# Expert up-projection with products of 448 columns, its halves added afterwards

## The chip, the cores and the metric

One core of one Trainium2 chip. The metric is the device time of one execution in microseconds (us); lower is better. The core's engines each work through a queue of their own: TensorE (PE, matrix products; PEld is its weight load), VectorE (DVE), ScalarE (ACT), GpSimd (POOL) and SyncE (SP, which here issues transfers). They wait for each other by semaphores.

## The reference

Two transformer blocks, one after the other, over 256 tokens of 1024 features. The change lies in the first block's expert layer (PEER). Each token gets 16 of 16384 experts from each of eight heads; an expert is a row of `peer_u` and a row of `peer_v`:

```
def expert_block(args):
    ht, it, gt = args
    ue = jnp.take(u, it, axis=0)
    act = jax.nn.gelu(jnp.einsum('tkd,td->tk', ue, ht), approximate=False)
    ve = jnp.take(v, it, axis=0)
    return jnp.einsum('tk,tkd->td', gt * act, ve)
```

## The kernel before

**Split products.** Every float32 operand a is cut into a high part a_h (rounded to the fast matmul type) and a low part a_l = a - a_h. A product a b is made as a_h b_h + a_h b_l + a_l b_h, three matrix products into one bank of PSUM; `three` issues them. The weight comes in *units* of 128 x 1024 values: SyncE loads a unit into one of four buffers `raw`, ScalarE makes its high part (`hi`, into one of three buffers `whi`, line L1234), and VectorE (`lo`, L1829) or GpSimd (L2777) makes the low part (`wlo`). Unit i's `hi` waits until TensorE has finished unit i - 3 (semaphore `w`).

**The expert layer is dense.** All 16384 experts are computed for 224 of the 256 tokens (`TD`; the first 32 tokens are done with gathered rows). The up-projection has 128 units ("u", unit 0 to 127), each 128 experts. TensorE works a unit in eight steps k (blocks of 128 features), each of them three products of 224 columns, the weight's part being loaded and the tokens' part `hT` being streamed: `whi` with the high tokens, `whi` with the low tokens, `wlo` with the high tokens. Two units share one bank, and three banks (4, 5, 6) take turns. ScalarE then applies GELU to both units of a bank at once (448 columns), into the buffer `acts` (inside `A2`, "A" in the profile). The down-projection ("v") follows, again 128 units; there `down` uses, for six of eight k, one product of 448 columns that streams both halves of the tokens' operand, and accumulates them in one place for each half; it adds the halves at the very end.

**Work beside it.** While TensorE does the up-projection, VectorE does the routing: `routing(0)` and then `routing(1)`, a generator each, cut into 30 pieces. Each engine's program steps its generators once per unit (twice in units 12, 26, 40 and 54, `U1_STEPS`), so a piece stands at a fixed place in the queue, but nothing except semaphores holds engines at the same unit. A routing is: the 16 largest of 128 for 16 rows (maxima, replacing them, maxima again, their indices; pieces 1 to 10), candidate sums (11), the 16 largest of 256 for eight rows (12 to 21), small conversions (22), the selection of indices by one-hot products and reductions (23 to 26), and normalised gates (27), for which ScalarE makes an exponential in piece 22. TensorE transposes the results after unit 27 and unit 55, and VectorE copies them (`iT`). In units 0 to 51 GpSimd makes the low parts, from then on VectorE. From unit 50 on GpSimd issues gathers for the first 32 tokens, and VectorE makes products with the gathered rows (`pick_u`; in unit 51 it also scales a row of tokens). From unit 70 on VectorE builds one-hot matrices in groups (`gates`), one group for two units, and TensorE multiplies them.

Of the kernel before, what the change touches and what calls it, by code (L numbers as in the profile page):

```python
# [7 lines left out]
ALU = mybir.AluOpType  # L8
ACT = mybir.ActivationFunctionType
# [29 lines left out]
NGRP = TD // OB  # L39
EARLY = 10  # L40
G_DENSE = 70
REP_AT = 51
DOT_AT = [55 + 3 * g // 2 for g in range(EARLY)] + [71 + 2 * (14 * g // 11) for g in range(NPK - EARLY)]
ACC_AT = [57 + 2 * g for g in range(NPK)]
# [125 lines left out]
hd_pe hd_act hd_dve hd_pool mask xv_ev cr_pe cr_act cr_dve  # L170
ff_a ff_c ff_g ff_h ff_lo
own_act own_dve own_pool zeros x_sq hi_half lo_half lo_first f_xg f_xd f_act hd_mask
pk_idx pk_rep pk_used pk_act v_tile v_b v_sum v_tr x_g
""".split()


# [37 lines left out]
def build(nc, x, mem, wdram, keep_d, con0_d, con1_d, con2_d, keys_d, w2c_d, gf_d, gf2_d,  # L214
          gffn_d, utab, out):
    ctx = ExitStack()
    with ctx:
# [25 lines left out]
        iota_b = sb("iota_b", P * 2, F16)  # L243
        zero_b = sb("zero_b", P, BF16)
        first_cut = sb("first_cut", 4 * T, F32R)

        with ExitStack() as c:
            A1 = sb("A1", 24576, c=c)
# [135 lines left out]

        def cut(part, n):
            return both_cuts(n)[:, part, :]

        v_banks = (0, 1, 2, 3, 5, 6, 4, 4)
        out_banks = ((7, 0), (1, 2))
# [77 lines left out]
        def pe_program(e):  # L467
# [136 lines left out]
            def lin_T(u0, units, src, K, first=None, after=None, steps=(1,), c0=0):  # L604
                per = KD // K
                for u in range(units):
                    i = u0 + u
                    wv = [z.rearrange("p (n k c) -> p n k c", n=per, k=K) for z in unit(i)]
                    for j in range(per):
                        n = u * per + j  # L610
                        q = pair[0]
                        bk = 4 + q % 3
                        if n % 2 == 0:
                            use(bk)
                        for k in range(K):
                            if n == 0 and first:
                                first(k)
                            ins = three(banks[bk][:, (n % 2) * 256:(n % 2 + 1) * 256 - c0], [z[:, j, k, :] for z in wv],
                                        [z[:, k, c0:T] for z in src], k == 0, k == K - 1)
                            if 2 * (j * K + k + 1) == KD:  # L620
                                mid.step()
                        if n % 2:
                            by, n_ev = PAIR_FREED[q]
                            free[bk] = (s[by], n_ev)
                            pair[0] += 1
                    ins.then_inc(s["w"], 1)
                    if after:
                        after(u)
                    side.step(steps[(i + 1) % len(steps)])

            def lin_A(u0, src, K, N, bks, ready, pair=True, split=None):
# [460 lines left out]
                    ins.then_inc(s["sc_pe"], 1)  # L1092
                    free[g] = (s["sc_act"], 4 * b + g + 1)
            side.lists[0] += [routing(0), routing(1)]
            lin_T(BASE["u"], 62, hTv, KD, steps=U1_STEPS, c0=NG)
            side.drain()
            lin_T(BASE["u"] + 62, G_DENSE - 62, hTv, KD, c0=NG)
            side.lists[0] += [gates(0), gates(1)]
            lin_T(BASE["u"] + G_DENSE, P - G_DENSE, hTv, KD, c0=NG)

            def down(n, w, k):
                bk, o = banks[v_banks[k]], v_cols(k) + NG
# [125 lines left out]
        def act_program(e):  # L1228
# [449 lines left out]
                    act(hrep[q, :], hrep[0:NG, :], ACT.Copy).then_inc(s["pk_rep"], 1)  # L1678

            side.lists[0] += [routing(0), routing(1)]  # L1680
            lin_T(BASE["u"], 62, gelu(0), rep_h, steps=U1_STEPS)
            side.drain()
            def first_cuts(u):
                if u == 64:
                    cut_acts(0)
                    cut_acts(1)

            lin_T(BASE["u"] + 62, 66, gelu(62), first_cuts)
            e.wait_ge(s["pk_used"], NPK)
            act(pk_co, pk_dot, ACT.Gelu).then_inc(s["pk_act"], 1)  # L1690
            for n in range(128):
# [123 lines left out]
        def dve_program(e):  # L1815
# [848 lines left out]
            own(e.tensor_copy(banks[7][:, 0:16], K_("iota16")))  # L2664
            own(e.tensor_copy(t3(iota_b[:, :], P), K_("iota").unsqueeze(2).to_broadcast([P, P, 2])))
            side.lists[0] += [routing(0), routing(1)]
            lin_T(BASE["u"], 62, before=pick_u, steps=U1_STEPS)
            side.drain()
            lin_T(BASE["u"] + 62, G_DENSE - 62, before=lambda u: pick_u(u + 62))
            side.lists[0] += [gates(0), gates(1)]  # L2670
            lin_T(BASE["u"] + G_DENSE, P - G_DENSE, before=lambda u: pick_u(u + G_DENSE))
            cut_acts(0)
            cut_acts(1)
            for n in range(128):
# [425 lines left out]
```

## Time and profile before

| | |
|---|---|
| median of three runs | 1383.48 us (1383.48 to 1385.43) |
| profiled execution | 1383.28 us, its span 1381.2 us |
| TensorE busy | 1357.3 us, 98% of the span |
| VectorE busy | 1037.8 us, 75% |
| ScalarE busy | 737.3 us, 53% |
| GpSimd busy | 292.4 us, 21% |

The span is the time from the first to the last instruction on the core; the execution's own time is 2.1 us longer. Busy time counts an engine's instructions once, where they overlap. A single product's length includes its way through the array, and products overlap, so what one costs in a stream is read from the distance between starts. "Granted clock" is the share of 2.4 GHz that TensorE got.

### The profile page before, as it was taken

How to read it: one execution, taken by the hardware profiler on the slowest of the kernel's cores; microseconds unless marked ns; L12 is line 12 of the kernel's file. 1: busy time of each engine (PE TensorE's matmuls, PEld its weight loads, DVE VectorE, ACT ScalarE, POOL GpSimd, SP SyncE). 2: the span in 40 equal slices, each digit the busy share in tenths (PEclk: the TensorE clock that was granted, in tenths of full speed). 3: DMA queues.
4: the chain of work that ended last, by engine and by line, in shares of the span. 5: the costliest groups of instructions: out<-in, count | busy, mean ns of one | idle time of the engine just before them, and what ended most of it. 6: DMA issues, size and time to landing. Idle time of an engine off the chain costs nothing.

```text
span 1381.2 us, 26739 instructions
## 1 busy us (share of the span) xinstructions
PE 1357.3 (98%) x10949; PEld 1290.1 (93%) x10949; DVE 1037.8 (75%) x1850; ACT 737.3 (53%) x1077; POOL 292.4 (21%) x176
## 2 busy tenths in 40 slices
PE   9999999999999999999999999999999999999997
PEld 7989989999999999999999999999898798899985
DVE  5556575593987899999999878987787664777744
ACT  5674645545464444444444455555677554655533
POOL 6000000288873222220000033220232000100000
PEclk9999999999999999999999999999999999999999
DMA  6433366456569867775555689987443543555552
GB/s 247 144 131 128 120 197 214 139 199 198 196 221 326 287 238 253 245 253 183 187 184 191 197 323 345 350 301 241 139 141 107 182 153 118 172 184 187 187 190 92
DMA packets 76586, 279.26 MB, mean 202 GB/s; under 512 B 8497, under 2 KB 8753, under 8 KB 76209
## 3 DMA queue, kind: packets, MB, share of 16 engines
q1 hardware_dynamic: 67104, 243.73, 52.8%
q0 software_dynamic: 9216, 33.56, 6.5%
q8 instruction: 87, 1.43, 0.4%
q14 instruction: 35, 0.28, 0.1%
q10 hardware_dynamic: 144, 0.26, 0.1%
HBM read 276.47 MB, written 1.05 MB: 201 GB/s over the span
## 4 chain that ended last, share of the span: by engine, by line
PE 75%; issue 15%; ACT 4%; DVE 4%; POOL 1%; DMA 0%; POOLq 0%; SPq 0%; DVEq 0%; ACTq 0%
PE bank L478 74%; ACT A L1234 2%; DVE wlo L1829 1%; ACT whi L1234 1%; PE bank L487 1%; POOL wlo L2777 1%; ACT L1234 1%; DVE A L1829 1%; DVE A L1825 0%; DMA xres<-in_x 0%; DVE xres L1829 0%; ACT hT L1234 0%; DVE small L2575 0%; DVE A L1826 0%; POOL small L2783 0%
## 5 line engine op out<-in xcount | busy, mean ns | idle before, releaser
L478 PE MATMUL bank<-hT,whi 128*128 128x224 f32 (+2 forms) x5148 | 1008.8, 294 | 2.6 <-DVE wlo L1829 1.7
L478 PEld LDWEIGHTS bank<-hT,whi 128*128 128x128 f32 x5148 | 811.5, 190 | 18.8 <-DVE wlo L1829 2.5
L478 PE MATMUL bank<-hT,wlo 128*128 128x224 f32 (+1 forms) x2952 | 810.8, 275 | 0.0
L1234 ACT ACTIVATE whi<-raw 128x1024 fp32r<-128x1024 f32 (+1 forms) x450 | 473.3, 1053 | 354.9 <-PE bank L478 344.9
L1829 DVE TENSOR_TENSOR wlo<-raw,whi 128x1024 fp32r<-128x1024 f32 (+1 forms) x385 | 471.8, 1227 | 227.3 <-ACT whi L1234 227.0
L478 PEld LDWEIGHTS bank<-hT,wlo 128*128 128x128 f32 x2952 | 562.7, 191 | 0.0
L1234 ACT ACTIVATE A<-bank 128x512 f32<-128x512 f32 (+4 forms) x170 | 90.1, 537 | 217.8 <-PE bank L478 208.2
L2777 POOL TENSOR_TENSOR wlo<-raw,whi 128x1024 fp32r<-128x1024 f32 x63 | 150.6, 2409 | 156.7 <-ACT whi L1234 154.1
L2793 POOL DMA_INDIRECT A<-in_v,small x32 | 50.4, 1576 | 288.2 <-DVE A L1825 174.1
L2783 POOL TENSOR_TENSOR small<-small 128x1 f32<-128x1 f32 x14 | 7.8, 558 | 483.8 <-DVE small L1826 480.1
L2793 POOL DMA_INDIRECT A<-in_utab,small x32 | 54.4, 1701 | 132.6 <-DVE A L1832 131.1
L478 PE MATMUL bank<-A 128*128 128x128 f32 (+9 forms) x472 | 69.9, 305 | 0.0
L478 PEld LDWEIGHTS bank<-A 128*128 128x128 f32 (+4 forms) x472 | 59.4, 182 | 6.4 <-issue 2.5
L1829 DVE TENSOR_TENSOR hT<-A,hT 128x224 fp32r<-128x224 f32 x126 | 48.4, 385 | 0.0
L1234 ACT ACTIVATE hT<-A 128x224 fp32r<-128x224 f32 x126 | 47.1, 375 | 0.0
L1832 DVE SCALAR_TENSOR_TENSOR A<-bank,A 128x512 f32<-128x512 f32 (+1 forms) x68 | 44.0, 657 | 2.2 <-PE bank L478 2.1
L1234 ACT ACT_TABLE_LOAD x34 | 43.6, 1283 | 2.2 <-PE bank L478 0.9
L1832 DVE SCALAR_TENSOR_TENSOR A<-A 128x1024 f32<-128x1024 f32 x33 | 40.3, 1220 | 1.9 <-ACT A L1234 1.9
L1829 DVE TENSOR_TENSOR og<-og_eq,gate 128x1024 f16<-128x1024 f16 x56 | 38.8, 692 | 1.9
L1832 DVE SCALAR_TENSOR_TENSOR A<-A,small 128x1024 f32<-128x1024 f32 x31 | 39.7, 1280 | 0.0
L478 PE MATMUL bank<-whi,R3h 128*128 128x512 f32 (+1 forms) x98 | 39.4, 402 | 0.0
L478 PE MATMUL bank<-wlo,R3h 128*128 128x512 f32 (+1 forms) x98 | 38.2, 390 | 0.0
(183 smaller groups left out, 1292.0 us busy)
## 6 DMA issues: line engine op xcount, KB each, us to landing
raw<-in_u SPq DMA_DIRECT2D x128, 512.0 KB, 3.4
raw<-in_v SPq DMA_DIRECT2D x128, 512.0 KB, 4.0
raw<-in_w_up SPq DMA_DIRECT2D x44, 512.0 KB, 3.3
raw<-in_w_down SPq DMA_DIRECT2D x22, 512.0 KB, 3.3
raw<-in_w_in_t SPq DMA_DIRECT2D x17, 512.0 KB, 3.9
raw<-in_w_in_g SPq DMA_DIRECT2D x16, 512.0 KB, 3.3
raw<-in_w_out SPq DMA_DIRECT2D x16, 512.0 KB, 4.1
raw<-in_w_pq SPq DMA_DIRECT2D x16, 512.0 KB, 4.2
```

The lines of the kernel that those rows point to most:

```text
L478: return e.matmul(o, l, r, start=st, stop=sp_, skip_group_check=True)
L487: return e.transpose(o, i, ident[0:k, 0:k])
L1234: return e.activation(o, i, func, **kw)
L1829: return e.tensor_tensor(o, a, b, op)
L1832: return e.scalar_tensor_tensor(o, a, z, b, op0, op1, **kw)
L2777: e.tensor_tensor(l, raw[i % NRAW][:, :], h.bitcast(F32), ALU.subtract).then_inc(s["lo_pool"], 1)
L2783: e.tensor_tensor(st[:, 2:3], st[:, 3:4], mhalf, ALU.pow).then_inc(s["n_rstd"], 1)
L2793: e.indirect_dma_start(out=pk_buf(g), out_offset=None, in_=table, in_offset=bass.IndirectOffsetOnAxis(ap=pk_idx[:, i:i + 1], axis=0)).then ...
```

## The change

In units 0 to 125 of the up-projection one product of 448 columns streams the high and the low tokens behind each other with `whi`, and one of 224 columns adds `wlo` with the high tokens onto the first half. A unit so fills a bank alone, with two halves that must still be added. ScalarE copies the second half into the idle buffer `first_cut` (`take_low`; two places take turns), and then

- in the 32 units 4 to 19 and 32 to 47 (`ADDED`) VectorE adds bank and copy into `acts`, and ScalarE's GELU reads and writes it there;
- in the other 94 units TensorE adds the copy onto the bank's first half, by a product with the identity in the middle of the next unit (`join`, ahead of k = 4), and the GELU reads the bank.

Each unit has a GELU of its own, two units later in ScalarE's queue. Units 126 and 127 are done as before. The core of the diff:

```diff
+NWIDE = 126
+JOIN_AT = 4
+ADDED = [n for n in range(56) if n % 28 in range(4, 20)]
...
+        def u_part(n):
+            return first_cut[:, (2 + n % 2) * T:(2 + n % 2) * T + TD]
+
+        def u_whole(n):
+            done = sum(k <= n for k in ADDED)
+            return (s["u_sum"], done) if n in ADDED else (s["u_join"], n + 1 - done)
+
+        def u_freed(n):
+            if n in ADDED:
+                return u_whole(n)
+            return (s["ev_act"], PAIR_FREED[PAIR["u"] + n // 2][1]) if n % 2 else (s["u_even"], n // 2 + 1)
...
+            def join(n):
+                e.wait_ge(s["u_low"], n + 1)
+                mm(banks[4 + n % 3][:, 0:TD], ident_r[:, :], u_part(n), False, True).then_inc(s["u_join"], 1)
+
+            def wide(u0, u1, steps=(1,)):
+                both = t4(hT[:, :], 2, KD)
+                for u in range(u0, u1):
+                    i = BASE["u"] + u
+                    wv = two(unit(i), KD)
+                    bk = banks[4 + u % 3]
+                    use(4 + u % 3)
+                    for k in range(KD):
+                        if k == JOIN_AT and u and u - 1 not in ADDED:
+                            join(u - 1)
+                        mm(bk[:, 0:2 * TD], wv[0][:, k, :], both[:, :, k, NG:T], k == 0, False)
+                        ins = mm(bk[:, 0:TD], wv[1][:, k, :], both[:, 0, k, NG:T], False, False)
+                        if 2 * (k + 1) == KD:
+                            mid.step()
+                    ins.then_inc(s["w"], 1)
+                    free[4 + u % 3] = u_freed(u)
+                    pair[0] += u % 2
+                    side.step(steps[(i + 1) % len(steps)])
...
-            lin_T(BASE["u"], 62, hTv, KD, steps=U1_STEPS, c0=NG)
+            e.wait_ge(s["ident_r"], 1)
+            wide(0, 62, U1_STEPS)
...
+            def take_low(n):
+                if n >= 2:
+                    e.wait_ge(*u_whole(n - 2))
+                e.wait_ge(s["w"], BASE["u"] + n + 1)
+                act(u_part(n), banks[4 + n % 3][:, TD:2 * TD], ACT.Copy).then_inc(s["u_low"], 1)
+
+            def gelu_one(n):
+                if TD * (n + 1) > 15872:
+                    e.wait_ge(s["rt_dve"], 8)
+                if TD * (n + 1) > 16896:
+                    e.wait_ge(s["pk_used"], EARLY)
+                e.wait_ge(*u_whole(n))
+                act(acts[:, n, :], acts[:, n, :] if n in ADDED else banks[4 + n % 3][:, 0:TD], ACT.Gelu).then_inc(s["ev_act" if n % 2 else "u_even"], 1)
+                pair[0] += n % 2
+
+            act(ident_r[:, :], ident, ACT.Copy).then_inc(s["ident_r"], 1)
+            for u in range(P):
+                if 0 < u <= NWIDE:
+                    take_low(u - 1)
+                hi(BASE["u"] + u + 2)
+                if 2 <= u < NWIDE + 2:
+                    gelu_one(u - 2)
...
+            def add_low(u):
+                n = u - 1
+                if n in ADDED:
+                    e.wait_ge(s["u_low"], n + 1)
+                    tt(acts[:, n, :], banks[4 + n % 3][:, 0:TD], u_part(n).bitcast(F32), ALU.add).then_inc(s["u_sum"], 1)
+                pick_u(u)
```

On TensorE, the end of unit 1 and the start of unit 2 before the change (`x2` is two products in a row; `bank4` and `bank5` are PSUM banks, `whi` and `wlo` a unit's parts):

```order
L478 MATMUL bank4<-hT,whi2 128x224 x2
L478 MATMUL bank4<-hT,wlo2 128x224
L478 MATMUL bank5<-hT,whi0 128x224 x2
L478 MATMUL bank5<-hT,wlo0 128x224
L478 MATMUL bank5<-hT,whi0 128x224 x2
```

Now, in unit 1, with the identity product for unit 0 in its middle, and the start of unit 2:

```order
L494 MATMUL bank5<-hT,whi2 128x448
L494 MATMUL bank5<-hT,wlo2 128x224
L494 MATMUL bank4<-first_cut,ident_r 128x224
L494 MATMUL bank5<-hT,whi2 128x448
L494 MATMUL bank5<-hT,wlo2 128x224
...
L494 MATMUL bank6<-hT,whi0 128x448
L494 MATMUL bank6<-hT,wlo0 128x224
```

A k has two products instead of three, a bank is left after one unit instead of two, and one product of the unit before stands between.

On ScalarE, the start of the up-projection before (`A2<-bank0` to `bank3` are copies of the routing scores, `A2<-bank4` and on the GELUs):

```order
L1234 ACTIVATE A2<-bank3 128x512
L1234 ACTIVATE whi0<-raw0 128x1024
L1234 ACTIVATE whi1<-raw1 128x1024
L1234 ACT_TABLE_LOAD
L1234 ACTIVATE A2<-bank4 128x448
L1234 ACTIVATE whi2<-raw2 128x1024
L1234 ACTIVATE whi0<-raw3 128x1024
L1234 ACTIVATE A2<-bank5 128x448
```

And now:

```order
L1275 ACTIVATE A2<-bank3 128x512
L1275 ACTIVATE ident_r<-keep 128x128
L1275 ACTIVATE whi0<-raw0 128x1024
L1275 ACTIVATE first_cut<-bank4 128x224
L1275 ACTIVATE whi1<-raw1 128x1024
L1275 ACTIVATE first_cut<-bank5 128x224
L1275 ACTIVATE whi2<-raw2 128x1024
L1275 ACT_TABLE_LOAD
L1275 ACTIVATE A2<-bank4 128x224
L1275 ACTIVATE first_cut<-bank6 128x224
```

The identity's copy stands ahead of the first `hi`, a copy stands ahead of every `hi` from then on, and the first GELU stands behind unit 4's `hi` with the table load before it.

On VectorE, the second routing's first pieces and the sums of units 32 and 33 (`bank6`, `bank4`), as they stand now; before the change the same rows stand without the two that read `first_cut`:

```order
L2161 MAX A2<-A2 128x8 x16
L2168 MATCH_REPLACE A2<-A2 128x128 x16
L2175 MAX A2<-A2 128x8 x8
L1897 TENSOR_TENSOR A2<-bank6,first_cut 128x224
L2175 MAX A2<-A2 128x8 x8
L1897 TENSOR_TENSOR A2<-bank4,first_cut 128x224
L2182 MAX_INDEX A2<-A2 128x8
```

Five pieces stand ahead of the first sum, and one piece between a sum and the next.

## Rows read from the trace of the kernel before

**Rows 1.** The page's busy times (us, share, count) and TensorE's granted clock.

```profile
PE 1357.3 (98%) x10949; PEld 1290.1 (93%) x10949; DVE 1037.8 (75%) x1850; ACT 737.3 (53%) x1077; POOL 292.4 (21%) x176
...
PEclk9999999999999999999999999999999999999999
```

**Rows 2.** Busy us (count) by stretch, then clock, DMA share, GB/s.

```profile
263.00:452.00 189.00, 188.83 (x1691) 188.65 (x1690) 154.85 (x500) 99.66 (x116) 142.10 (x65) 1.00 0.66 224
452.00:622.00 170.00, 170.00 (x1829) 169.37 (x1829) 155.87 (x216) 73.96 (x89) 42.52 (x22) 1.00 0.73 252
```

**Rows 3.** TensorE's timeline in the up-projection: start us, length us, what.

```profile
300.09 0.39 PE L478 MATMUL bank<-hT,whi 128*128 128x224 f32 x2
...
302.10 0.39 PE L478 MATMUL bank<-hT,whi 128*128 128x224 f32 x2
```

**Rows 4.** TensorE's timeline in the down-projection.

```profile
902.08 0.38 PE L478 MATMUL bank<-hT,whi 128*128 128x448 f32 x1
...
903.97 0.39 PE L478 MATMUL bank<-hT,whi 128*128 128x224 f32 x2
...
904.64 0.60 PE L487 MATMUL bank<-keep,A 128*128 128x128 f32 x4
```

**Rows 5.** Groups by line and shape, whole run: busy us, mean ns, idle before.

```profile
L1234 ACT ACTIVATE hT<-A 128x224 fp32r<-128x224 f32 x126 | 47.1, 375 | 0.0
...
L1829 DVE TENSOR_TENSOR A<-A,bank 128x256 f32<-128x256 f32 x22 | 9.1, 414 | 0.0
```

**Rows 6.** ScalarE's timeline; in brackets the idle time before, and its releaser.

```profile
263.45 0.60 ACT L1234 ACTIVATE A<-bank 128x512 f32<-128x512 f32 x1 [0.30 <-PE bank L478]
263.94 1.05 ACT L1234 ACTIVATE whi<-raw 128x1024 fp32r<-128x1024 f32 x1
...
393.92 1.28 ACT L1234 ACT_TABLE_LOAD   x1
...
396.49 1.28 ACT L1234 ACT_TABLE_LOAD   x1
```

**Rows 7.** VectorE's timeline, between the two routings and through the second.

```profile
338.81 0.56 DVE L2173 COPY iT<-bank 128x384 f32<-128x384 f32 x1 [17.67 <-PE bank L487]
...
340.20 2.39 DVE L1829 TENSOR_TENSOR gate<-iT,gate 128x128 f16<-128x128 f32 x1
342.51 0.17 DVE L1832 SCALAR_TENSOR_TENSOR small<-A 32x32 f32<-32x32 f32 x1
...
342.81 2.30 DVE L1832 SCALAR_TENSOR_TENSOR small<-A 32x32 f32<-32x32 f32 x1
...
348.08 3.18 DVE L2093 MAX8 A<-A 128x8 f32<-128x128 f32 x16
...
355.60 3.19 DVE L2107 MAX8 A<-A 128x8 f32<-128x128 f32 x16
...
367.31 2.40 DVE L2127 CAST A<-A 128x256 f32<-128x256 uint32 x1
...
387.49 0.73 DVE L1825 TENSOR_SCALAR A<-A 128x128 uint32<-128x128 uint32 x2
...
388.67 2.48 DVE L1829 TENSOR_TENSOR bank<-A,bank 128x512 f32<-128x512 f32 x4
...
404.65 2.32 DVE L1829 TENSOR_TENSOR wlo<-raw,whi 128x1024 fp32r<-128x1024 f32 x1 [2.29 <-ACT whi L1234]
```

**Rows 8.** GpSimd's timeline, low parts of the weights.

```profile
340.05 2.39 POOL L2777 TENSOR_TENSOR wlo<-raw,whi 128x1024 fp32r<-128x1024 f32 x1 [0.62 <-ACT whi L1234]
...
403.48 2.40 POOL L2777 TENSOR_TENSOR wlo<-raw,whi 128x1024 fp32r<-128x1024 f32 x1
```

**Rows 9.** TensorE's timeline at the start of unit 53.

```profile
405.94 0.48 PE L478 MATMUL bank<-hT,whi 128*128 128x224 f32 x2 [0.17 <-POOL wlo L2777]
```

**Rows 10.** VectorE's timeline in the one-hot stage, two units apart.

```profile
542.04 1.22 DVE L1829 TENSOR_TENSOR wlo<-raw,whi 128x1024 fp32r<-128x1024 f32 x1 [0.17 <-ACT whi L1234]
...
547.97 1.23 DVE L1829 TENSOR_TENSOR wlo<-raw,whi 128x1024 fp32r<-128x1024 f32 x1 [0.16 <-ACT whi L1234]
```

More of the change, by code:

```diff
@@ L172 @@
 own_act own_dve own_pool zeros x_sq hi_half lo_half lo_first f_xg f_xd f_act hd_mask
-pk_idx pk_rep pk_used pk_act v_tile v_b v_sum v_tr x_g
+pk_idx pk_rep pk_used pk_act v_tile v_b v_sum v_tr u_low u_sum u_join u_even ident_r x_g
 """.split()
@@ L245, in build @@
         first_cut = sb("first_cut", 4 * T, F32R)
+        ident_r = sb("ident_r", P, F32R)
         with ExitStack() as c:
@@ L1094, in pe_program @@
             side.lists[0] += [routing(0), routing(1)]
-            lin_T(BASE["u"], 62, hTv, KD, steps=U1_STEPS, c0=NG)
+            e.wait_ge(s["ident_r"], 1)
+            wide(0, 62, U1_STEPS)
             side.drain()
-            lin_T(BASE["u"] + 62, G_DENSE - 62, hTv, KD, c0=NG)
+            wide(62, G_DENSE)
             side.lists[0] += [gates(0), gates(1)]
-            lin_T(BASE["u"] + G_DENSE, P - G_DENSE, hTv, KD, c0=NG)
+            wide(G_DENSE, NWIDE)
+            lin_T(BASE["u"] + NWIDE, P - NWIDE, hTv, KD, lambda k: join(NWIDE - 1) if k == JOIN_AT else None, c0=NG)
             def down(n, w, k):
@@ L1680, in act_program @@
             side.lists[0] += [routing(0), routing(1)]
[L1681 to L1684, printed above, removed]
+            def take_low(n):
[18 more added lines that the diff above has]
+                    gelu_one(u - 2)
+                if u < 62:
+                    rep_h(u)
+                    side.step(U1_STEPS[(BASE["u"] + u + 1) % len(U1_STEPS)])
+                    if u == 61:
+                        side.drain()
+                    continue
+                if u == 126:
                     cut_acts(0)
                     cut_acts(1)
-            lin_T(BASE["u"] + 62, 66, gelu(62), first_cuts)
+                side.step()
+            e.wait_ge(s["w"], BASE["u"] + P)
+            gelu(NWIDE)(0, t3(banks[4 + pair[0] % 3][:, :], 2))
+            pair[0] += 1
             e.wait_ge(s["pk_used"], NPK)
@@ L2666, in dve_program @@
             side.lists[0] += [routing(0), routing(1)]
-            lin_T(BASE["u"], 62, before=pick_u, steps=U1_STEPS)
+            def add_low(u):
[4 more added lines that the diff above has]
+                pick_u(u)
+            lin_T(BASE["u"], 62, before=add_low, steps=U1_STEPS)
             side.drain()
@@ L2671, in dve_program @@
             lin_T(BASE["u"] + G_DENSE, P - G_DENSE, before=lambda u: pick_u(u + G_DENSE))
+            e.wait_ge(*u_whole(NWIDE - 1))
             cut_acts(0)
```

## The prediction

> **What bounds the kernel now.** I read the page first: TensorE is busy for 98% of the span at the full granted clock, VectorE for 75% [rows 1]. The busy time by stretch then says which engine is close behind it where the change works: from 263 to 622 us (the up-projection of the experts) TensorE is never idle for more than a fraction of a microsecond, and VectorE is busy 82%, later 92% [rows 2]. So a shorter product stream shortens the kernel, as long as nobody becomes late.
>
> TensorE's timeline gives the price of a product. In the up-projection one k is three products of 224 columns, and six k take 302.10 - 300.09 = 2.01 us, 0.335 us each [rows 3]; a unit of eight is 2.68 us. The down-projection, further on in this same kernel, already has the wide form: six k of 448 + 224 columns take 903.97 - 902.08 = 1.89 us, 0.315 each, and the two k after them in three products take 904.64 - 903.97 = 0.67 us, 0.335 each again [rows 4]. Both forms stream 672 columns, 0.280 us at 2.4 GHz. What differs is about 0.02 us for each product that isn't issued.
>
> **What is removed.** Units 0 to 125 lose one product per k: 126 x 8 x 0.020 = 20.2 us. Bounds: the rows are read to 0.01 us, so 0.0185 to 0.021 each, 18.6 to 21.2 us.
>
> **What is added on TensorE.** 126 - 32 = 94 units get a product with the identity, of 224 columns. A third of 0.335 is 0.112 us, so 10.5 us. At the least it is its columns alone at 2.4 GHz, 0.093 us, 8.8 us; at the most it breaks the stream as a change to another kind of product does, for which I allow 0.02 us more, 12.4 us. I take 10.5, since the down-projection changes its bank at every k at no cost that shows [rows 4]. A unit now takes 8 x 0.315 = 2.52 us, or 2.63 with an identity product. Net of both: 9.7 us less.
>
> A rule of the Trainium skill speaks against the change: "TensorE: Matmul & The Clock Gate", section "Back-to-back issue gap", has a product follow the last one after its columns at 2.4 GHz plus about 2.5 ns. By that rule 1008 merged products would give back 2.5 us and 94 identity products cost 9.0 us, a net loss of 6.5 us before any wait. The rows show about 18 ns over the columns for each product, not 2.5, so the sum goes by them.
>
> **What is added on the other engines.** ScalarE had one GELU of 448 columns for two units (0.55 us). Now each unit has a copy of the low half and a GELU of its own, about 0.37 us each by a like row [rows 5], and the next instruction starts 0.1 us before an end. Its split of the weights (`hi`, 1.06 us) stays. About 1.6 us in a unit of 2.6 are hidden, unless order makes them late: a bank is now full after one unit, so three banks are a ring of three units instead of six. In the steady state unit n's bank is free after the end of unit n+1 plus 0.26 us (signal), 0.27 (copy), 0.97 (`hi`), 0.36 (GELU) and a signal, some 1.95 us; TensorE wants it after 2.63. Slack 0.7 us, no cost. VectorE adds 32 sums of 224 columns, each 0.3 to 0.4 us (0.41 for 256 columns with one source in a bank [rows 5]). They cost TensorE nothing by themselves. But each waits for its unit's low half, so VectorE, which ran far ahead of TensorE, walks beside it in units 5 to 20 and 33 to 48. Behind a waiting sum stand VectorE's pieces of the routing (and from unit 52 on its own `lo`, for which TensorE waits two units later); behind ScalarE's GELU of a summed unit, which waits for the sum, stand the next unit's copy and `hi`, and GpSimd's `lo` after that; behind an identity product that waits stands the second half of its unit.
>
> **Where someone is late.** I follow the queues with the rows' durations; unit u of before starts at 263.2 + 2.68u, and 0.35 later from unit 28 on, for the transposes ahead of it.
>
> (1) Unit 0 waits for the identity's copy, which ScalarE does behind the eight score copies. The last began at 263.45 and let the next start at 263.94 [rows 6]; plus 0.3 us it is 264.25 instead of 263.2. Cost 1.0 us.
>
> (2) The first GELU loads its table (1.28 us [rows 6]). It was hidden by a free bank; now unit 3 wants unit 0's bank, 2.63 us after the start of unit 2, and gets it at 0.26 + 0.27 + 0.97 + 1.28 + 0.36, some 3.25. Cost 0.65 us. Two softmax exponentials (unit 20 and unit 48) bring two loads each [rows 6]. ScalarE is then 1.1 us late, and the low half for the second identity product comes about 0.3 us after TensorE wants it. Cost 0.3 us each.
>
> (3) The first routing keeps up. Its pieces of 1.4 to 2.1 us plus a sum fit into 2.52 us. The two that don't (about 3.3 us, before units 11 and 13) are followed by short ones. TensorE's transposes come after unit 27, and VectorE was done 18 us early [rows 7].
>
> (4) The second doesn't quite. VectorE gets its indices after those transposes at about 337.9 instead of 338.8, and took 9.3 us from there to its next search (348.08), because three tiny operations (340.20, 342.81 and one more like them) took 2.3 us each where a twin (342.51) takes 0.2 [rows 7]; GpSimd was at its `lo` then, 2.4 us long [rows 8]. Five pieces of the search (348.08 to the middle of the maxima of 355.60, 9.1 us) come before the first sum: it is done at 337.9 + 9.3 + 9.1 + 0.3 = 356.6. Unit 33 starts at 264.25 + 33 x 2.52 + 16 x 0.112 (identity products) + 0.65 + 0.3 (waits) + 0.35 (transposes), 350.5, and unit 35 wants the bank of unit 32 two plain units later, 355.5. Cost 1.1 us. After it VectorE makes 2.4 us a unit against 2.52. If the integer-to-float cast takes 2.4 us again instead of 0.3 [rows 7], 1.7 us more. Price at the ends: 0 (no tiny operation stuck) to 3 us.
>
> (5) The worst place is units 53 to 55. VectorE began the selection of the second routing at 388.7, that is 3.5 us before unit 48 started (392.2) [rows 7], and yet TensorE was 0.36 us late at unit 53 (405.94 instead of 405.6, 0.17 of it idle), for GpSimd's last `lo`, 403.48 to 405.88 [rows 8, 9]. Now unit 47's sum (done 1.0 us after the start of unit 48) and the 1.2 us of small steps from 387.49 on hold it back to 2.2 us after that start. From there the selection (two times four and four operations of 512, 5.0 us, and one reduction of 2.3 us between), the scaled row (1.5) and `lo` of unit 54 (1.2, or 2.3 as in 404.65 [rows 7]) end 17.2 to 18.3 us after that start; TensorE wants it after 2.52 + 5 x 2.63 = 15.7 us, plus 0.3 for the exponential and 0.35 to 1.05 for GpSimd's last `lo`, 16.4 to 17.1. The reduction of 2.3 us and `lo` of unit 55 add 0.8. Cost 1.5 to 3.1 us, I take 2.3, less the 0.36 us that was lost there before.
>
> (6) From unit 70 on VectorE builds one-hot groups. Two units take it about 5.77 us of 5.93 [rows 10], and TensorE's pair becomes 5.83. It keeps up by 0.06 us. If it didn't, up to 28 x 0.1 = 2.8 us of the gain would be lost.
>
> Waits: 1.0 + 0.65 + 0.6 + 1.1 + 2.3 - 0.35 = 5.3 us. Change: -9.7 + 5.3 = -4.4 us. The profiled execution of before took 1383.28 us for its span of 1381.2 us, and the median of the runs is 1383.48. So 1383.3 - 4.4 = 1378.9.
>
> **The rivals.** Likeliest, 0.55: as above, waits of 3 to 7.5 us: 1376.5 to 1381.
>
> VectorE is not late, 0.20: steps (4) and (5) cost next to nothing, since the tiny operations meet no GpSimd work or the sums are quicker. Waits 2 us, 1383.3 - 7.7 = 1375.6. For: twins of 0.2 us stand in the same rows. Against: GpSimd's share grows as units shorten.
>
> VectorE is late everywhere, 0.15: cast and `lo` stuck too, the one-hot stage at its limit: 3 + 3.1 + 2.8 + 2.3 - 0.35, about 11 us of waits, 1384.5. Against: all three must fall badly in one kernel. For: the cast and `lo` did so in the rows.
>
> The ring of three banks binds, 0.05, slower: if the chain from a unit's end to its freed bank is 2.75 us instead of 1.95, each of 94 units waits 0.12 us, 11 us in all: 1390. It decides from 2.63 us on. Nothing in the rows makes ScalarE's steps that long, but no row has its order of copy, `hi`, GELU.
>
> The merge saves nothing here, 0.05, slower: in the down-projection every k has another bank, here all are in one; if the 0.02 us came from that, the identity products and waits alone remain, 1383.3 + 10.5 + 5.3 = 1399. Against: the three-product k have the same 0.335 us with changing and with fixed bank. The skill's 2.5 ns ("TensorE: Matmul & The Clock Gate", same section) would land in this case, near 1395.
>
> **The numbers.** About 0.2% (2.8 us) is what a measurement can tell from no change. Below 1380.7: four fifths of the likeliest and all of the second, 0.64. Within: the rest of the likeliest and most of the third, 0.23. Slower: the last two and a little of the third, 0.13. Range 1375.0 to 1385.0: it leaves out the two slower cases and the tails. The likeliest case's own range is 1376.5 to 1381.
>
> **What the profile after would show.** In the up-projection: 448 + 224 columns every 0.315 us (0.335 would refute the saving); a unit every 2.52 or 2.63 us; no table load beyond the five there; TensorE idle about 1 us at 263, 0.65 us before unit 3, and for VectorE's sums or `lo` at unit 35 and units 53 to 55; VectorE without idle time from 349 to about 420; pairs of 5.83 us from unit 70. If TensorE idles before every unit instead, the ring is the cause; if VectorE has idle time at unit 53, my step (5) is wrong.

## The result, and the profile after

The changed kernel takes 1387.11 us (median of 15 runs, 1385.63 to 1387.93) against 1383.89 us for the kernel before (15 runs, 1383.45 to 1386.83). The ratio is 1.0016, 95% interval 1.0009 to 1.0023: 0.16% slower, where 1378.9 us was forecast (0.3% faster). The profiled execution took 1387.66 us for a span of 1385.6.

The page, compared with [rows 1]: TensorE has 915 products fewer and is still busy as long.

```profile
PE 1356.4 (98%) x10034; PEld 1264.3 (91%) x10035; DVE 1051.0 (76%) x1882; ACT 773.8 (56%) x1267; POOL 288.9 (21%) x176
```

To see where the time went I took two marks that both kernels have: the last score copy of ScalarE (263.45 in [rows 6]) and the first product of the down-projection (624.28 us before). Before, the stage between them took 360.83 us. In the changed kernel the marks are at 264.28 and 627.12: 362.84 us. So the stage that was to give 4.4 us costs 2.0. TensorE's timeline of the changed kernel shows all of it (start us, length us, what, in brackets the idle time before and who ended it):

```profile
265.12 0.47 PE L494 MATMUL bank<-hT,whi 128*128 128x448 f32 x1 [0.89 <-ACT ident_r L1275]
...
273.75 0.44 PE L494 MATMUL bank<-hT,whi 128*128 128x448 f32 x1 [0.49 <-ACT A L1275]
...
298.63 0.38 PE L494 MATMUL bank<-hT,whi 128*128 128x448 f32 x1
...
301.19 0.38 PE L494 MATMUL bank<-hT,whi 128*128 128x448 f32 x1
...
322.54 0.37 PE L494 MATMUL bank<-first_cut,ident_r 128*128 128x224 f32 x1 [1.02 <-ACT first_cut L1275]
...
325.44 0.37 PE L494 MATMUL bank<-first_cut,ident_r 128*128 128x224 f32 x1
...
358.90 0.27 PE L494 MATMUL bank<-hT,wlo 128*128 128x224 f32 x1
359.81 0.44 PE L494 MATMUL bank<-hT,whi 128*128 128x448 f32 x1 [0.65 <-DVE A L1897]
...
398.15 0.37 PE L494 MATMUL bank<-first_cut,ident_r 128*128 128x224 f32 x1 [1.02 <-ACT first_cut L1275]
...
408.30 0.47 PE L494 MATMUL bank<-hT,whi 128*128 128x448 f32 x1 [0.30 <-POOL wlo L2853]
...
412.03 0.47 PE L494 MATMUL bank<-hT,whi 128*128 128x448 f32 x1 [0.82 <-DVE wlo L1897]
...
415.36 0.48 PE L494 MATMUL bank<-hT,whi 128*128 128x448 f32 x1 [0.41 <-DVE wlo L1897]
...
545.53 0.28 PE L494 MATMUL bank<-first_cut,ident_r 128*128 128x224 f32 x1
...
551.43 0.28 PE L494 MATMUL bank<-first_cut,ident_r 128*128 128x224 f32 x1
...
627.12 0.45 PE L494 MATMUL bank<-first_cut,whi 128*128 128x448 f32 x1
```

**The price of a k.** Between 298.63 and 301.19 lie eight k of units whose halves VectorE adds: 2.56 us, 0.320 us a k. Six k of the same form in the down-projection of the kernel before took 0.315 [rows 4]. The merge gives 0.015 us per k against the old 0.335, 1008 x 0.015 = 15.1 us, not 20.2.

**The price of the identity.** In units with an identity product ScalarE's steps are 2.67 us apart, so the product costs 0.11 (0.107 over many units of the fourth experiment below): 94 x 0.107 = 10.1 us, as forecast (10.5).

**The waits.** The idle times in brackets sum to 5.6 us. A restart costs more than the idle time: the first wide product after one takes 0.44 to 0.48 us instead of 0.38, and its start is 0.91 us behind the last product's at 358.90 where 0.10 is usual. So the 0.65 us there cost 0.87. Counted that way, by the distances between starts, the eight waits and the two identity products that come late behind them (325.44 and the one at 401.05) cost about 7.9 us: 1.0 at the first unit, 0.7 at 273.75, 1.5 each at the two exponentials, 0.9 at 359.81 and 2.3 at units 53 to 55. The balance is -15.1 + 10.1 + 7.9 - 0.36 (the wait of [rows 9], gone) = +2.5, and +2.0 was measured. It closes to half a microsecond, of which 0.2 lies at the stage's very end (from the last one-hot products to the first product of the down-projection it was 0.93 us before and is 0.70 now).

The rest of the profiled run's +4.4 lies outside the stage. It reached the first mark 0.83 us later (across the runs below that mark lies between 263.3 and 264.3, whatever the kernel), and after 988 us TensorE ran for a few microseconds at a mixture of its two clock levels (columns: stretch, its length, busy us (count) of TensorE, its loads, VectorE, ScalarE, GpSimd, then granted clock, DMA share, GB/s):

```profile
983.00:988.00 5.00, 3.12 (x25) 2.92 (x25) 4.12 (x10) 3.42 (x4) 4.82 (x9) 1.00 0.31 105
988.00:993.00 5.00, 5.00 (x30) 5.00 (x31) 5.00 (x10) 0.35 (x1) 0.29 (x2) 0.66 0.59 190
```

Its 24 products there take 4.64 us in the chain of the changed kernel, and 3.11 in that of the kernel before:

```profile
987.98 4.64 PE bank L494 x24
```

```profile
985.13 3.11 PE bank L478 x24
```

TensorE had been idle for nearly the same time just ahead in both (1.20 and 1.78 us now, 1.21 and 1.79 before). The lower clock cost 1.5 us there (4.64 - 3.11). Executions of both kernels fall into two groups 1.7 to 2.0 us apart (nine of 15 in the upper one now, seven of 15 before), so the medians differ by 3.2 us, but the kernels within either group by 1.9 to 2.1, as in the stage. I compare the stage in what follows.

**Who was late.** ScalarE's timeline at unit 21 has the largest wait:

```profile
319.38 1.28 ACT L1275 ACT_TABLE_LOAD   x1
321.93 0.31 ACT L1275 ACTIVATE A<-A 128x128 f32<-128x128 f32 x1 [1.27 <-DVE A L1897]
322.15 0.34 ACT L1275 ACTIVATE first_cut<-bank 128x224 fp32r<-128x224 f32 x1
```

The table is loaded by 320.66, but the exponential begins at 321.93: it waits for VectorE's piece 22, and behind it stands the low half's copy at 322.15, for which TensorE's identity product waits until 322.54. The same happens at 397.54. Piece 22 is late for two reasons. It stands behind the sum of its own unit, and its conversion of integers took 2.45 us, from just after the start to just after the end of one `lo` of GpSimd:

```profile
319.25 2.45 DVE L2213 CAST A<-A 128x256 f32<-128x256 uint32 x1
```

```profile
319.16 2.39 POOL L2853 TENSOR_TENSOR wlo<-raw,whi 128x1024 fp32r<-128x1024 f32 x1 [0.16 <-ACT whi L1275]
```

The same conversion took 0.29 us in experiment 4 below. At that length it would have been done, by an estimate from these rows, at about 319.8, ahead of the table.

VectorE's timeline in the second routing:

```profile
340.77 0.56 DVE L2241 COPY iT<-bank 128x384 f32<-128x384 f32 x1 [1.68 <-PE bank L503]
...
344.90 2.39 DVE L1900 SCALAR_TENSOR_TENSOR small<-A 32x32 f32<-32x32 f32 x1
...
347.42 0.18 DVE L1900 SCALAR_TENSOR_TENSOR small<-A 32x32 f32<-32x32 f32 x1
...
350.21 3.18 DVE L2161 MAX8 A<-A 128x8 f32<-128x128 f32 x16
...
359.30 0.37 DVE L1897 TENSOR_TENSOR A<-bank,first_cut 128x224 f32<-128x224 f32 x1
...
394.87 2.44 DVE L2213 CAST A<-A 128x256 f32<-128x256 uint32 x1
...
397.43 2.48 DVE L1897 TENSOR_TENSOR bank<-A,bank 128x512 f32<-128x512 f32 x4
...
410.76 1.21 DVE L1897 TENSOR_TENSOR wlo<-raw,whi 128x1024 fp32r<-128x1024 f32 x1
```

From the copy of the indices to the next search it took 9.4 us, with three tiny operations of 2.3 to 2.4 us again (the forecast had 9.3). The first sum of the second routing ends at 359.67 and lets unit 35 start at 359.81. The cast at 394.87 was stuck too (2.44 us); it is what the second exponential waits for. The `lo` for unit 54 ends at 411.97, when TensorE has waited 0.82 us.

### The profile page after: what moved, and what is told of

Same layout as the page of the kernel before. It is cut to its first block, busy times and chain, and to the rows that moved or that the text cites. A ratio compares the mean times of both kernels' runs of the same rounds, so it can differ in the third digit from the quotient of the medians.

```text
span 1385.6 us, 25348 instructions
## 1 busy us (share of the span) xinstructions
PE 1356.4 (98%) x10034; PEld 1264.3 (91%) x10035; DVE 1051.0 (76%) x1882; ACT 773.8 (56%) x1267; POOL 288.9 (21%) x176
## 4 chain that ended last, share of the span: by engine, by line
PE 72%; issue 15%; DVE 7%; ACT 4%; POOL 1%; DMA 0%; SPq 0%; POOLq 0%; ACTq 0%; DVEq 0%
PE bank L494 71%; ACT A L1275 2%; DVE wlo L1897 2%; ACT whi L1275 1%; DVE A L1897 1%; PE bank L503 1%; ACT L1275 1%; POOL wlo L2853 1%; DMA raw<-in_w_in_t 0%; DVE A L1893 0%; DVE small L1900 0%; DVE A L2213 0%; DVE bank L1897 0%; DVE A L2168 0%; DVE xres L1897 0%
## 5 line engine op out<-in xcount | busy, mean ns | idle before, releaser
L494 PE MATMUL bank<-hT,whi 128*128 128x256 f32 (+2 forms) x4140 | 998.6, 323 | 6.0 <-DVE wlo L1897 2.9
L494 PE MATMUL bank<-hT,wlo 128*128 128x224 f32 (+1 forms) x2952 | 801.0, 271 | 0.0
L494 PEld LDWEIGHTS bank<-hT,whi 128*128 128x128 f32 x4140 | 695.3, 189 | 40.8 <-DVE wlo L1897 4.3
L1275 ACT ACTIVATE A<-bank 128x224 f32<-128x224 f32 (+3 forms) x201 | 88.5, 446 | 126.3 <-PE bank L494 116.7
L1275 ACT ACTIVATE first_cut<-bank 128x224 fp32r<-128x224 f32 x126 | 45.1, 358 | 144.0 <-PE bank L494 144.0
L2869 POOL DMA_INDIRECT A<-in_utab,small x32 | 50.8, 1586 | 136.9 <-DVE A L1900 135.3
L1275 ACT ACTIVATE A<-A 128x224 f32<-128x224 f32 (+6 forms) x81 | 42.3, 536 | 7.7 <-DVE A L1897 6.9
```

The costliest lines, as they stand in the source:

```text
L494: return e.matmul(o, l, r, start=st, stop=sp_, skip_group_check=True)
L1275: return e.activation(o, i, func, **kw)
L2869: e.indirect_dma_start(out=pk_buf(g), out_offset=None, in_=table, in_offset=bass.IndirectOffsetOnAxis(ap=pk_idx[:, i:i + 1], axis=0)).then ...
```

## The experiments

Unless said otherwise, the edit is to the changed kernel, and the stage is the time between the two marks.

**1. Another bank for every other k.**

```
 for k in range(KD):
+    odd = u >= G_DENSE and k % 2 == 1
+    to = banks[7] if odd else bk
-    mm(bk[:, 0:2 * TD], wv[0][:, k, :], ...
+    mm(to[:, 0:2 * TD], wv[0][:, k, :], ...
```

From unit 70 on the odd k go to bank 7, so their products are missing from the output.

> In units 70 to 125 the odd k go to the free bank 7 instead of the unit's bank, so that each k changes the bank, as in the down-projection; what bank 7 holds is not used, so half of these units' sum is left out. Bank theory (a k of 448 + 224 columns costs 0.320 us here and 0.315 there because here all eight write one bank): two units from unit 70 on take about 0.07 us less than in the changed kernel, 0.315 us a k; 28 pairs give about 1.5 to 2 us less. Rival (the two stages differ in something else: the tokens' columns, the other engines' traffic): the k stays at 0.320 us.

It took 1386.77 us (one run), stage 362.89. ScalarE's splits, two units apart in the one-hot stage:

```profile
546.61 1.05 ACT L1277 ACTIVATE whi<-raw 128x1024 fp32r<-128x1024 f32 x1
...
552.50 1.05 ACT L1277 ACTIVATE whi<-raw 128x1024 fp32r<-128x1024 f32 x1
```

A pair still takes 5.89 us (5.90 in the changed kernel). That all k share one bank is not what costs the 0.005 us.

**2. Other columns of the tokens' operand.** Both kernels stream columns 32 to 255 of each row of 256, the tokens that aren't gathered. The down-projection's operand starts at column 0.

```
-mm(bk[:, 0:2 * TD], wv[0][:, k, :], both[:, :, k, NG:T], ...
+mm(bk[:, 0:2 * TD], wv[0][:, k, :], both[:, :, k, 0:TD], ...
-ins = mm(bk[:, 0:TD], wv[1][:, k, :], both[:, 0, k, NG:T], ...
+ins = mm(bk[:, 0:TD], wv[1][:, k, :], both[:, 0, k, 0:TD], ...
```

The output is that of other tokens.

> The wide units stream the tokens' columns 0 to 223 instead of 32 to 255, which start where a block starts, as in the down-projection; the activations are thus those of other tokens. If the start of the streamed operand made the difference, a k takes 0.315 us in units 0 to 125, and the time is 1008 x 0.0045, 4.5 us, less. The bank theory expects 0.320 us and no change.

Eight k take 2.52 us, 0.315 each:

```profile
298.79 0.38 PE L494 MATMUL bank<-hT,whi 128*128 128x448 f32 x1
...
301.31 0.38 PE L494 MATMUL bank<-hT,whi 128*128 128x448 f32 x1
...
360.48 0.44 PE L494 MATMUL bank<-hT,whi 128*128 128x448 f32 x1 [3.12 <-DVE A L1897]
```

But the time is 1387.88 us (one run) and the stage 363.19: the faster TensorE waits 3.12 us instead of 0.65 for VectorE's first sum in the second routing, where four small operations between 340.46 and 348.68 took 2.3 to 2.4 us each this time, instead of three. A second loss follows the wait. From 362 to 365 us the granted clock was 0.50, the lower of its two levels (1.2 GHz), and the k there took 0.58 us, which cost another 1.6 us (the columns are those of the row at 983 above):

```profile
362.00:365.00 3.00, 3.00 (x13) 2.78 (x12) 3.00 (x22) 0.76 (x3) 2.37 (x1) 0.50 0.02 10
```

After the wait of 0.65 us in the changed kernel no stretch of this stage had less than full clock. So the price of a k is explained by the operand's place, and here the gain was taken back by the wait for VectorE and by the clock after it.

**3. No joining at all.** No identity product and no sum; the low half of units 0 to 125 is copied but left out of the result.

```
-ADDED = [n for n in range(56) if n % 28 in range(4, 20)]
+ADDED = []
...
-    return (s["u_sum"], done) if n in ADDED else (s["u_join"], n + 1 - done)
+    return (s["u_low"], n + 1)
...
-if k == JOIN_AT and u and u - 1 not in ADDED:
+if False:
```

So a GELU waits only for the low half's copy.

> The wide products stay, but nothing adds the halves: neither identity products nor VectorE's sums; the copy of the low half stays, the low half is left out of the result. It measures the merge alone, with the ring of three banks. By the trace of the changed kernel a unit takes 8 x 0.320 = 2.56 us, so 126 x 0.12 = 15.1 us less than before; waits for the identity's copy (1.05), the GELU's table (0.65) and around the exponentials (at most 1) stay, VectorE's walking goes. Stage 12 to 13.5 us shorter than before, time 1370 to 1372 us. If the ring itself costs TensorE time at every unit, it comes out above 1375.

1373.38 us (one run), stage 350.97, 9.9 us less than before the change, where 12 to 13.5 were expected. A unit takes 2.56 us throughout, so neither the ring of three banks nor ScalarE's longer list costs anything per unit. By the price of a k the stage would be 360.83 - 15.1 - 0.36 = 345.4; 5.6 us of waits remain even here: 0.88 at the first unit, 0.59 at the first GELU, two of 1.16 at the exponentials, and 0.27 and 0.51 at units 53 and 55 (idle times, without the restarts). So the exponentials cost more than was expected, and at 2.56 us a unit GpSimd's and VectorE's `lo` come late there even when VectorE adds nothing.

**4. The identity everywhere.** Only `ADDED = []`: 126 identity products, no sums by VectorE.

> All 126 units use the identity product, VectorE adds nothing and runs ahead again. Theory (VectorE's walking beside TensorE makes the waits at unit 35, 53, 54 and 55, and part of those at units 21 and 49): 32 products more cost 32 x 0.11 = 3.5 us, and some 4 us of waits go, so the time is that of the changed kernel, 1385 to 1387. Rival (those waits come from the order in ScalarE's and GpSimd's queues): they stay, and the time is 3.5 us above the changed kernel, about 1390.

1385.76 us (10 runs), ratio 1.0015 (1.0005 to 1.0024), stage 362.50. The waits at unit 35 and at units 53 to 55 are gone. Four are left, 0.88, 0.49 and two of this kind:

```profile
401.34 0.44 PE L494 MATMUL bank<-hT,whi 128*128 128x448 f32 x1 [0.95 <-ACT A L1275]
```

The 32 sums save 32 x 0.107 = 3.4 us of TensorE and cost about as much in waits: adding on VectorE where it is busy is worth nothing.

**5. Sums in the first routing only.** `ADDED = list(range(4, 20))`.

> The changed kernel with the sums by VectorE in units 4 to 19 only; units 32 to 47 get an identity product as well. If the waits at unit 35 (0.65 us idle) and units 53 to 55 (0.30, 0.82, 0.41) come from VectorE walking beside TensorE through the second routing, they shrink to nothing, and 16 more identity products cost 16 x 0.109 = 1.7 us: 2.2 + 0.6 of restarts less 1.7 is about 1 us less, 1386.0 us, against 1387.1 for the changed kernel and 1385.8 for all units with identity products. If those waits have another cause (the second routing itself, one unit shorter than before), they stay at about 2 us and the time is 1388.5.

1385.48 us (10 runs, before on the same chip 1384.79; ratio 1.0007, 0.9997 to 1.0016), stage 361.12: 1.7 us less than the changed kernel, 1.4 less than with no sums. The waits at units 35 and 53 to 55 are gone here too; the first routing's sums make nobody late but by the exponential:

```profile
322.18 0.37 PE L494 MATMUL bank<-first_cut,ident_r 128*128 128x224 f32 x1 [1.02 <-ACT first_cut L1275]
```

**6. Two starts moved, identity everywhere.** The identity's copy goes ahead of the eight score copies, and ScalarE makes a GELU of one column in unit 0.

```
 lin_T(BASE["w_pq"], 16, copy_to(qT))
+act(ident_r[:, :], ident, ACT.Copy).then_inc(s["ident_r"], 1)
...
 hi(BASE["u"] + u + 2)
+if u == 0:
+    act(small[:, 252:253], ident[:, 0:1], ACT.Gelu)
```

> Identity products in all units, and two starts moved: ScalarE copies the identity ahead of the eight score copies, and makes one dummy GELU of one column in unit 0, where it has slack, so that the table is there at unit 3. If the 0.88 us at the first unit and the 0.49 us at unit 3 are the copy and the table load, both go (with their restarts about 1.5 us), and 1385.8 us becomes 1384.3, the stage 362.5 becomes 361.0. If the start is held back by something else that ends at the same time (the score copies themselves), only the 0.49 goes: 1385.3.

The stage is 360.66, 1.8 us less than in experiment 4, and TensorE isn't idle at 264 and 273 any more. The median is 1384.96 us (nine runs; a tenth took 2175.95 us), ratio 1.0001 (0.9992 to 1.0011). What remains:

```profile
323.25 0.44 PE L494 MATMUL bank<-hT,whi 128*128 128x448 f32 x1 [0.95 <-ACT A L1275]
...
399.39 0.44 PE L494 MATMUL bank<-hT,whi 128*128 128x448 f32 x1 [0.95 <-ACT A L1275]
```

**7. Sums only where VectorE has idle time.** As experiment 6, with the first exponential one unit later and the sums in 34 other units:

```
-ADDED = [n for n in range(56) if n % 28 in range(4, 20)]
+ADDED = list(range(21)) + [25, 26] + list(range(58, 69))
...
-for _ in range(21):
+for _ in range(21 + (b == 0)):
...
-lin_T(BASE["u"] + 62, G_DENSE - 62, before=lambda u: pick_u(u + 62))
+lin_T(BASE["u"] + 62, G_DENSE - 62, before=lambda u: add_low(u + 62))
```

> As the kernel before it, with the first exponential one unit later, and VectorE adds the halves where it has idle time: units 0 to 20, 25 and 26, and 58 to 68 (34 units), none in the second routing. If a sum costs TensorE nothing where VectorE idles, 34 x 0.109 = 3.7 us less than the kernel before it, and the exponential's wait at unit 21 (0.94) is gone: 1384.3 - 3.7 - 0.5 to 0.9 = about 1380, faster than the kernel before the change by some 3.5 us. If every sum makes someone late, or the single bank's chain (half copied, summed, GELU) binds in the stretch from unit 58 on, waits of 0.1 us a unit or more come back and it stays at 1383 to 1385.

1380.58 us (6 runs, 1379.00 to 1382.29) against 1384.79, ratio 0.9968 (0.9956 to 0.9980): faster than both kernels. The stage is 356.06 us. TensorE's groups in it (line, engine, what, count, busy us, mean ns, idle before and for whom) have one wait left, and no identity product waits:

```profile
L494 PE MATMUL bank<-hT,whi 128*128 128x448 f32 x1007 | 330.2, 381 | 0.9 <-ACT A L1275 0.9
...
L494 PE MATMUL bank<-first_cut,ident_r 128*128 128x224 f32 x92 | 26.0, 283 | 0.0
```

ScalarE's exponential no longer waits for VectorE behind its table:

```profile
319.17 1.28 ACT L1275 ACT_TABLE_LOAD   x1
320.46 0.31 ACT L1275 ACTIVATE A<-A 128x128 f32<-128x128 f32 x1
```

By the terms found above it is 360.83 - 15.1 + 92 x 0.107 + 1.1 (one wait with its restart) - 0.36 = 356.3; 356.06 was measured.

**8. The same with columns 0 to 223**, as in experiment 2 (the output is that of other tokens).

> The kernel before it, with the products of the up-projection streaming columns 0 to 223 in place of 32 to 255 (the output is that of other tokens). If the first streamed column makes the 0.005 us of a k, units take 2.52 and 2.63 us, 1008 x 0.005 = 5.0 us less, about 1375, less what VectorE then lacks in time: it needed 5.77 us for a pair from unit 70 on against 5.81, and was within 0.1 us of being late, so 1375 to 1377. If VectorE's one-hot groups bind instead, the pair stays at 5.89 and about 3 of the 5 us are lost: 1378.

1377.50 us (2 runs), ratio 0.9948 (0.993 to 0.9966), stage 353.00: 3.1 of the 5 us. Plain units take 2.52 us, and the identity products lie 5.84 us apart for a pair in the one-hot stage, as the forecast's 5.83, so VectorE keeps up there. A pair gains 0.06 us instead of 0.08, and new is a wait of 0.33 us for VectorE's `lo` at 408.35, about 0.5 with its restart.

```profile
547.56 0.27 PE L494 MATMUL bank<-first_cut,ident_r 128*128 128x224 f32 x1
...
553.40 0.27 PE L494 MATMUL bank<-first_cut,ident_r 128*128 128x224 f32 x1
```

**9 to 14. Which columns.** Six kernels like that of experiment 7, each run once, differ in the columns alone (with 33 and 64 the stream runs on into the next row, and the last k takes the first's; the last two stream 222 columns of 224). The output of each is that of other or fewer tokens.

> The version with sums in VectorE's idle time, its up-projection streaming columns 16 to 239 (64 bytes into each row of 256) in place of 32 to 255. If only a start at column 0 is free of the 0.005 us, a plain unit takes 2.56 us and the stage from the last score copy to the down-projection stays near 356.1. If what costs is that the stream runs up to the row's last column (255), it is 2.52 us and about 353.

> The same with columns 31 to 254, an odd start. If any start behind column 0 costs the same 0.005 us, a plain unit takes 2.56 us; if the cost grows with how far the start is off an even boundary, it is more than 2.56 (0.325 us a k and 2.60 a unit, if each operand line is touched twice); if the last column is what counts, 2.52.

> The same kernel, its up-projection streaming 224 columns from column 33 of tile k (k = 7 takes tile 0's), so that the stream begins one column after 32 and runs one column into the next tile's row. Starts at 0, 16 and 31 gave 2.52, 2.51 and 2.51 us a unit, the start at 32 gave 2.56. If a start at exactly 32 (a multiple of 32 columns behind the first) makes it, or an end at exactly 255, this one takes 2.51 and the stage about 351.3. If every start from 32 on costs, it is 2.56 and 356.

> The same with 224 columns from column 64 of tile k (k = 7 takes tile 0's), running 32 columns into the next tile. If a start at a multiple of 32 columns other than 0 is what costs, a unit takes 2.56 us here too; if an end at exactly 255 is what costs, or an output and operand that start 32 columns apart, it takes 2.51 to 2.52.

> The version with sums in VectorE's idle time, its up-projection streaming 222 columns, 32 to 253 of each part (the last two of 224 are left out). Fewer columns alone make a k 0.0025 us shorter. If the stream that begins at column 32 is what costs 0.005 us, a plain unit takes 2.54 us; if a stream that ends at the row's last column (255) is, it takes 2.49.

> The same with columns 34 to 255 (222 columns up to the row's end). Start at 32 costs: 2.49 us a unit here. End at 255 costs: 2.54.

A unit is the mean of seven plain ones, 281 to 299 us:

```
columns      unit us   stage us   time us
32 to 255    2.56      356.06     1380.58 (experiment 7)
0 to 223     2.52      353.00     1377.50 (experiment 8)
16 to 239    2.51      351.44     1374.23
31 to 254    2.51      350.88     1375.42
33 to 256    2.51      353.48     1378.19
64 to 287    2.52      352.97     1377.51
32 to 253    2.55      354.55     1377.60
34 to 255    2.51      351.28     1374.65
```

The last two tell it apart, here eight k of the one that begins at 32 (2.55 us) and then of the one that ends at 255 (2.51 us):

```profile
298.81 0.37 PE L494 MATMUL bank<-hT,whi 128*128 128x444 f32 x1
...
301.36 0.37 PE L494 MATMUL bank<-hT,whi 128*128 128x444 f32 x1
```

```profile
298.80 0.38 PE L494 MATMUL bank<-hT,whi 128*128 128x444 f32 x1
...
301.31 0.38 PE L494 MATMUL bank<-hT,whi 128*128 128x444 f32 x1
```

It is the start at column 32, not the row's end. My expectation that every start behind column 0 costs the same fell with experiments 9 and 10: in plain units 16, 31, 33 and 34 are the cheapest of all, and 64 is as 0.

The start isn't all of it, though. The kernel that starts at 33 has a stage of 353.48, 2 us more than the one at 16 with the same plain unit. In its units with an identity product the distances from one such product to the next alternate, here 2.62 and 2.69 us:

```profile
344.47 0.27 PE L494 MATMUL bank<-first_cut,ident_r 128*128 128x224 f32 x1
...
347.09 0.27 PE L494 MATMUL bank<-first_cut,ident_r 128*128 128x224 f32 x1
...
349.78 0.27 PE L494 MATMUL bank<-first_cut,ident_r 128*128 128x224 f32 x1
```

At 16 they are 2.62 throughout, at 32 2.67. So a start of 33 pays the higher price in every other unit of that kind. Why 32 is always dearer, and 33 sometimes, isn't shown.

## Why the prediction was wrong

Its net was -4.4 us; the stage went up by 2.0, a miss of 6.4. Two of its steps failed: the price of a k, taken from another operand, and the wait at the exponentials. It gave "slower" a chance of 0.13, mostly by a ring of banks that binds or a merge that saves nothing, and neither happened. By its own steps:

**What is removed: mis-sized, 5.1 us of the miss.** The step "both forms ... differ by about 0.02 us for each product that isn't issued" took the 0.315 us of a k from the down-projection and gave bounds of 18.6 to 21.2 us from the rounding of the rows. The mechanism was right, but the duration belongs to an operand that starts at column 0. The up-projection's starts at column 32 and takes 0.320: 15.1 us. The old form hid this, since a k of three products took 0.335 in both places. The bounds took in how exactly the row was read, not that the row was another operand's.

**What is added on TensorE: right.** 94 identity products cost 0.107 us each, 10.1 against 10.5. The prediction weighed a rule of the Trainium skill ("TensorE: Matmul & The Clock Gate", section "Back-to-back issue gap"), columns at 2.4 GHz plus about 2.5 ns. It left out what that section says of it: this is the gap of an isolated product, and in a stream of weight loads and products, as here, both set the distance. The trace agrees that the rule doesn't hold in this stream: as an estimate it would give 2.5 us for 1008 merged products, where 15.1 are measured, and 0.096 us for an identity product, where 0.107 is. The section's own figure for such a stream, about 131 ns a product of 512 columns, isn't borne out either: from the start of a product of 448 columns to the next it is 0.22 us here (298.63 to 298.85). By the rule the change loses 6.5 us before any wait; the runs show 5.0 gained before the waits and the loss in them, so that its sign came out right was luck.

**ScalarE's ring: right.** No cost in any unit (experiment 3), the rival that it binds is out. VectorE's sum takes 0.37 us, as forecast.

**Step (1): right.** 1.0 forecast, 0.89 idle and 0.1 of restart. **Step (2), first GELU: right**, 0.65 against 0.49 idle, 0.7 with the restart. Experiment 6 took both away.

**Step (2), exponentials: wrong, 2.4 us of the miss.** I wrote that ScalarE "is then 1.1 us late" and that this costs 0.3 us each. Only the table loads were in it. The exponential also waits for VectorE, which now arrives with the same unit because its sums hold it back, and whose conversion was stuck for 2.4 us both times (1.27 us in the row at 321.93). The copy behind it delays an identity product by 1.02 us and the next one by 0.15: about 1.5 us each, 3.0 instead of 0.6. The prediction knew of the stuck conversion, but priced it in step (4), outside its sum, and not in the exponential's wait. With the first exponential one unit later only 0.2 us is left there (experiment 7), so the table loads alone were priced well where sums stand ahead of them. Where none do, two waits of 0.95 us remain (experiment 4), at the start of a unit: there the GELU behind the second table load has to free a bank, which the prediction didn't follow.

**Step (3): right** as to TensorE's transposes and the pieces. Its one neighbour that waited was the exponential above.

**Step (4): right, 1.1 forecast, 0.65 idle or 0.87 with the restart.** Three small operations were stuck as in [rows 7]. How many are depends on where they fall beside GpSimd's `lo`, and so on TensorE's pace: the same stretch in experiment 1 gave 0.66 us, and with a faster TensorE it was 3.12 (experiment 2). That the forecast met it this closely is in part luck.

**Step (5): right.** 2.3 forecast; 0.30, 0.82 and 0.41 us idle, 2.3 with restarts. Experiments 4 and 5 show that the walking causes it: without sums in the second routing it is gone. At 2.56 us a unit part of it is back without any sum (experiment 3).

**Step (6): right.** A pair takes 5.90 us, 5.83 plus 16 x 0.005, and 5.84 with the cheaper columns.

So 5.1 for the merge and 2.4 for the exponentials, less 0.4 for the identity and 0.2 for step (4), make 6.9 us, where 6.4 was measured: the same half microsecond stays open as above. Against the medians, +3.2 us, the rest lies outside the stage, as said with the result; whether the change causes any of it isn't settled.

The range's top, 1385.0, came from VectorE being late everywhere. That case put all uncertainty into the waits and none into the price of a k, which enters 1008 times.

## What to carry to other kernels

A duration that is multiplied by a thousand should come from the very operand that will be used: the same product at another start column differed by 1.6%, and here that was a quarter of the forecast saving (5.1 of 20.2 us). Work moved to an engine that runs ahead costs little where that engine has idle time and ties it to the slower one where it has none, and then everything queued behind it (table loads, exponentials, the low parts of weights) turns into waits. So give the idle stretches the work and leave the full ones alone: the same two ways of adding, distributed by VectorE's idle time, with two starts moved and the first exponential one unit later, made the loss of 0.16% a gain of 0.32%.

## What the runs showed of the hardware

Streaming both halves of the tokens costs 0.320 us a k when the stream starts at column 32 of a row of 256 float32 values, 0.315 at 0 and 64, and 0.313 at 16, 31 and 34. At 33 it is 0.313 in plain units, and up to 0.32 in every other unit with an identity product. With three narrow products the start made no difference (0.335 us at column 32 and at 0).

A k of 666 columns took the same 0.313 us as one of 672 (34 to 255 against 16 to 239, so their starts differ too), which suggests that at its cheapest a k isn't bound by its columns. What bounds it was not tried.

Small operations of VectorE that read SBUF alone took 2.3 to 2.4 us instead of 0.2 to 0.3 when they began just behind a `lo` of GpSimd, and then ended just behind it (319.25 to 321.70 beside 319.16 to 321.55). The 32 sums of the changed kernel, which read a bank of PSUM as well, took 0.37 to 0.39 us throughout.

After a wait of 3.12 us TensorE's granted clock was 0.50 from 362 to 365 us (experiment 2); after the waits of up to 1.02 us in the stage of the changed kernel it stayed at 1.00. After two waits of 1.2 and 1.8 us close together it fell in some executions and not in others (0.66 from 988 to 993 in the changed kernel, 1.00 in the kernel before).
